# Load order, eviction order and small-step order around the compressed branch of a two-block transformer kernel

## The reference, cut to what matters

```
x = x + 0.5 * swiglu(rms(x, ffn1_norm), ffn1_wg, ffn1_wu, ffn1_wd)
h = rms(x, mix_norm)
q_a, g_a, kc, vc, ks, vs, kw, vw, q_b, k_b, v_b, gate_a, gate_b = split(h @ w_in)
y_a = nsa(q_a, g_a, kc, vc, ks, vs, kw, vw, cmpk_*, cmpv_*) @ w_branch_nsa
y_b = moba(q_b, k_b, v_b) @ w_branch_moba
x = x + (sigmoid(gate_a) * y_a + sigmoid(gate_b) * y_b) @ w_out
x = x + 0.5 * swiglu(rms(x, ffn2_norm), ...)

# in nsa, the compressed branch (k = kc, vc; 2 groups of 64 features):
blocks = windows of 32 tokens, stride 16, + pos_emb
kcb, vcb = gelu(flat(blocks) @ w1) @ w2 ;  kcb = rope(kcb)
p = masked_softmax(q @ kcb * scale);  o_cmp = p @ vcb, weighted by sigmoid(g_a)
```

## Time and profile before

| | |
|---|---|
| median of three runs | 2011.68 us |
| profiled execution, its own time | 2013.12 us |
| its span | 2011.3 us |
| mean granted TensorE clock | 0.976 |
| TensorE busy | 1900.3 us, 94% |
| VectorE busy | 1279.0 us, 64% |
| ScalarE busy | 1100.7 us, 55% |
| GpSimd busy | 109.8 us, 5% |
| DMA | 287.55 MB, mean 143 GB/s |

### The profile page before, as it was taken

One profiled execution on the slowest core, in us unless ns is written; L12 is line 12 of the kernel. 1 busy time (PEld: TensorE's weight loads), 2 busy tenths in 40 slices (PEclk: granted clock), 3 DMA queues, 4 the chain that ended last, 5 costly groups with the idle time before them and its releaser, 6 DMA issues.

```text
span 2011.3 us, 35976 instructions
## 1 busy us (share of the span) xinstructions
PE 1900.3 (94%) x14196; PEld 1694.4 (84%) x14196; DVE 1279.0 (64%) x2078; ACT 1100.7 (55%) x1940; POOL 109.8 (5%) x101
## 2 busy tenths in 40 slices
PE   6999999998799989999989999999999979999997
PEld 4969978876799787888889898889888879898886
DVE  4652354366734667876657587767776647688766
ACT  4372254284534556774446467755774435557753
POOL 3000000004000003200000010001000000010001
PEclk6999999999899999999989999999999979999999
DMA  7231233132223322555442255555554442245544
GB/s 297 95 127 64 103 128 124 66 127 90 79 85 115 103 91 82 188 189 189 158 158 106 85 183 194 188 188 180 181 185 188 155 160 87 104 168 188 187 171 165
DMA packets 41713, 287.55 MB, mean 143 GB/s; under 512 B 4737, under 2 KB 6033, under 8 KB 7793
## 3 DMA queue, kind: packets, MB, share of 16 engines
q1 hardware_dynamic: 39392, 278.15, 38.6%
q0 software_dynamic: 2192, 7.57, 1.1%
HBM read 284.65 MB, written 1.05 MB: 142 GB/s over the span
## 4 chain that ended last, share of the span: by engine, by line
issue 50%; PE 37%; DVE 5%; ACT 4%; POOL 3%; DMA 1%; DVEq 0%; POOLq 0%; ACTq 0%
PE bank L1864 7%; PE bank L1866 7%; PE bank L1865 7%; PE bank L1870 6%; PE bank L1871 3%; PE bank L2002 2%; PE bank L2021 2%; PE bank L1979 1%; ACT work L936 1%; POOL work L760 1%; DVE panels_lo L1272 1%; PE bank L1923 1%; DMA xT<-xin 1%; PE bank L1960 1%; PE bank L2013 1%
## 5 line engine op out<-in xcount | busy, mean ns | idle before, releaser
L1272 DVE TENSOR_TENSOR panels_lo<-raw_panels,panels_hi 128x1024 fp32r<-128x1024 f32 x472 | 581.0, 1248 | 249.2 <-ACT panels_hi L827 247.8
L827 ACT ACTIVATE panels_hi<-raw_panels 128x1024 fp32r<-128x1024 f32 x472 | 488.6, 1054 | 427.6 <-PE bank L1866 279.3
L1870 PE MATMUL bank<-acts,panels_hi 128*128 128x512 f32 x2032 | 714.5, 397 | 3.6 <-DVE xT L1614 1.7
L1871 PE MATMUL bank<-acts,panels_lo 128*128 128x256 f32 x2032 | 568.4, 280 | 0.0
L1870 PEld LDWEIGHTS bank<-acts,panels_hi 128*128 128x128 f32 x2032 | 381.3, 188 | 96.1 <-DVE xT L1614 1.9
L1871 PEld LDWEIGHTS bank<-acts,panels_lo 128*128 128x128 f32 x2032 | 383.3, 189 | 0.2
L1864 PE MATMUL bank<-panels_hi,acts 128*128 128x256 f32 x1024 | 298.8, 292 | 39.5 <-ACT token_major L1164 21.5
L1864 PE MATMUL bank<-acts,panels_hi 128*128 128x256 f32 (+1 forms) x976 | 300.6, 308 | 3.6 <-DVE xT L1614 1.4
L1865 PE MATMUL bank<-acts,panels_hi 128*128 128x256 f32 (+1 forms) x976 | 296.7, 304 | 0.0
L1866 PE MATMUL bank<-acts,panels_lo 128*128 128x256 f32 (+1 forms) x976 | 296.7, 304 | 0.0
L1865 PE MATMUL bank<-panels_lo,acts 128*128 128x256 f32 x1024 | 295.3, 288 | 0.0
(11 more groups left out here) (229 smaller groups left out, 1982.1 us busy)
## 6 DMA issues: line engine op xcount, KB each, us to landing
raw_panels<-weights SPq DMA_DIRECT2D x262, 1024.0 KB, 4.8
near_bias<-rpb POOLq DMA_DIRECT2D x16, 256.0 KB, 3.0
gates<-weights SPq DMA_DIRECT2D x2, 1024.0 KB, 10.5
xT<-xin POOLq DMA_DIRECT2D x4, 512.0 KB, 12.5
out<-xT SPq DMA_DIRECT2D x4, 256.0 KB, 2.2
gates<-consts POOLq DMA_DIRECT2D x1, 448.0 KB, 4.5
consts_sb<-consts POOLq DMA_DIRECT2D x1, 356.0 KB, 3.3
raw_panels<-weights SPq DMA_DIRECT2D x2, 128.0 KB, 2.3
```

The lines of the kernel that those rows point to most:

```text
L827: act.activation(slot_hi(n, a, b), raw_of(n, a, b), ACT.Copy).then_inc(hi_ready, 1)
L1272: dve.tensor_tensor(slot_lo(n, a, b), raw_of(n, a, b), slot_hi(n, a, b).bitcast(F32), ALU.subtract).then_inc(lo_ready, 1)
L1870: pe.matmul(bank.rearrange("p (c t) -> p c t", c=2), whi_, with_rest(xhi_), start=start, stop=False, skip_group_check=True)
L1871: return pe.matmul(bank[:, 0:T], wlo_, xhi_, start=False, stop=stop, skip_group_check=True)
```

## The change

There are four edits. SyncE's loop takes two neighbouring pairs of panels in exchanged order: kv0+2 is waited for before kv0+1, and m0 before kv0+3, so that m0 is loaded before kv0+3 and m0+2 before m0+1. ScalarE evicts `nsa_kv` 0 and `compress(0)` ahead of rounding m0, and `moba_qkv` 0, the compressed keys and `compress_gelu(1)` ahead of rounding m0+2. VectorE rotates the compressed keys ahead of the split of m0+2 and the low parts of the queries, and runs the second half of the compressed softmax ahead of the low parts of the `moba` queries and the split of m0+6. TensorE turns the token scale into columns ahead of the branch gates' product.

```
+        def freeing_order():
+            order = list(range(START2["panels"], START2["panels"] + L["panels"]))
+            for n in sorted(PLAIN - {NSA_G}):
+                i = order.index(n)
+                order[i:i + 2] = [n + 1, n]
+            return order
...
-            for n in range(START2["panels"], START2["panels"] + L["panels"]):
+            for n in freeing_order():
...
 # ScalarE
-            tokens("nsa_kv", 0, [m0])
+            tokens("nsa_kv", 0, [])
             compress_out(0)
+            round_panel(m0)
             tokens("nsa_kv", 1, [])
             compress_out(1)
             compress_gelu(0)
             b = TWO["turn_nsa"].at["turns"]
-            tokens("moba_qkv", 0, [m0 + 1, m0 + 2])
-            compress_gelu(1)
+            tokens("moba_qkv", 0, [m0 + 1])
             act.wait_ge(cm_pe, now(cm_pe, 1))
             act.activation(kct[0:32, 0:HD], banks[7][0:32, 0:HD], ACT.Copy).then_inc(cm_act, 1)
+            compress_gelu(1)
+            round_panel(m0 + 2)
...
 # VectorE
             split_panel(m0 + 1)
             b = TWO["turn_nsa"].at["turns"]
-            for tt in range(TT):
-                turns_lo(b + tt, b + tt - 2, q_turned(0, tt), q_turned(1, tt), HD ** -0.5)
-            split_panel(m0 + 2)
             dve.wait_ge(cm_act, now(cm_act, 1))
             rope(kct[0:32, 0:HD], kct[0:32, P:2 * P], 1, ...)
             dve.sem_inc(cm_dve, 1)
+            split_panel(m0 + 2)
+            for tt in range(TT):
+                turns_lo(b + tt, b + tt - 2, q_turned(0, tt), q_turned(1, tt), HD ** -0.5)
             split_panel(m0 + 3)
...
             b = TWO["turn_moba"].at["turns"]
-            for tt in range(TT):
-                turns_lo(b + tt, b + tt - 2, q_turned(0, TT + tt), q_turned(1, TT + tt), HD ** -0.5)
-            split_panel(m0 + 6)
             dve.wait_ge(cm_act, now(cm_act, 3))
...
             dve.tensor_tensor(heads, heads, bcast(cstat[:, 0:16], 2, NCMP), ALU.mult).then_inc(cm_dve, 1)
+            for tt in range(TT):
+                turns_lo(b + tt, b + tt - 2, q_turned(0, TT + tt), q_turned(1, TT + tt), HD ** -0.5)
+            split_panel(m0 + 6)
...
 # TensorE
             tok_panels("cmp_kv")
+            pe.wait_ge(rs_ready, now(rs_ready, 2))
+            for tt in range(TT):
+                o = pe.matmul(banks[7][:, T + 2 * tt:T + 2 * tt + 2], rs[:, tt * P:(tt + 1) * P], ident[:, 0:2], ...)
+            o.then_inc(rcol_turned, 1)
             n, s = TWO["nsa_g"].at["panels"], TWO["nsa_g"].at["steps"]
             take(s)
...
             o.then_inc(tick, 1)
-            pe.wait_ge(rs_ready, now(rs_ready, 2))
-            for tt in range(TT):
-                o = pe.matmul(banks[7][:, T + 2 * tt:T + 2 * tt + 2], rs[:, tt * P:(tt + 1) * P], ident[:, 0:2], ...)
-            o.then_inc(rcol_turned, 1)
```

More of the change, by code:

```diff
@@ L2238, in _ @@
             tok_panels("cmp_kv")
+            pe.wait_ge(rs_ready, now(rs_ready, 2))
+            for tt in range(TT):
+                o = pe.matmul(banks[7][:, T + 2 * tt:T + 2 * tt + 2], rs[:, tt * P:(tt + 1) * P], ident[:, 0:2],
+                              start=True, stop=True, skip_group_check=True)
+            o.then_inc(rcol_turned, 1)
             n, s = TWO["nsa_g"].at["panels"], TWO["nsa_g"].at["steps"]
@@ L2249, in _ @@
             o.then_inc(tick, 1)
-            pe.wait_ge(rs_ready, now(rs_ready, 2))
-            for tt in range(TT):
-                o = pe.matmul(banks[7][:, T + 2 * tt:T + 2 * tt + 2], rs[:, tt * P:(tt + 1) * P], ident[:, 0:2],
-                              start=True, stop=True, skip_group_check=True)
-            o.then_inc(rcol_turned, 1)
             def compress(j):
```

## The result

The changed kernel takes 1989.86 us, median of four runs (1986.45 to 1993.27), beside 2014.12 us for the kernel before in the same rounds (2008.0 to 2017.09): a ratio of 0.9878, 95% interval 0.9858 to 0.9898, some 24 us or 1.2% faster. A second set of rounds gave 1986.79 us beside 2011.84, ratio 0.988 (0.9855 to 0.9905). The profiled execution took 1988.07 us, its span is 1986.3 us, and the mean granted clock 0.982.

A forecast was written before the change was run, and what follows sets the result against it. TensorE, busy 94% of the span, was taken as the bound. Gains of 10.8 + 9.8, 1.1 + 2.4, 2.8 and 2 x 0.8 make 28.5 us, less 3.4 for new falls: 25, so 1987 us median, range 1980 to 1997.

The forecast's parts named there:

- The chain load, rounding, eviction, TensorE: Before `nsa_kv` 2: m0's late load holds its rounding, that the eviction, that TensorE; a 10.1 us wait in layer 1.
- The new waits: TensorE would newly wait on loads before `compress(1)` and `moba_qkv` 1, 1.5 to 2.2 us each.
- the walk: Step-by-step timing of loads, splits and evictions in both layers: `moba_qkv` 1 starts 10.8 and 9.8 us earlier.
- The wait before `compress(0)`: In layer 2, `compress(0)` is held by the eviction of `nsa_q` 1 behind the rounding of kv0+2, ending at 1606.3.
- The token scale: Turned before the branch-gate product: TensorE's 1.2 us wait goes, but loads of q0+1 and kv0 are issued 0.6 us later.
- The second pair works against the change: m0+1, needed a step before m0+2, is loaded after it; in the old order layer 1's 2.1 us wait would go.
- Compressed keys and softmax: Waits of 1.1 and 2.4 us on the compressed keys go, and the softmax edit gains 0.8 us a layer.
- Clock: Layer 2's falls to half clock go, gaining 2.8 us; new falls after the new waits cost 3.4, bounds 0 and 6.8.
- The waits move to the loads: Rival, chance 0.19: slow load pairs turn the long wait into two waits a layer; gain 18.3 or 16 us, time 1995.
- The ring of loads: Rival, chance 0.05: m0+1's load waits for m0's rounding and split, so steps run in series; 2013 to 2020 us.

The follow-up runs named there:

- the changed kernel's second trace: The changed kernel, no further edit, profiled again in a second set of rounds: 1986.79 us, ratio 0.9880 to the kernel before.
- without the small steps: Changed kernel with VectorE's old order, and ScalarE's compressed-keys copy and `moba_qkv` 0 eviction again behind rounding m0+2: 1991.50 us, ratio 0.9885.
- the kernel of the table's last row: Changed kernel with only the first load pair exchanged, TensorE's edit undone, `moba_qkv` 5 eviction and probabilities copy ahead of rounding m0+7: 1979.06 us, ratio 0.9833.

## Why the prediction was right

- *The chain load, rounding, eviction, TensorE.* This mechanism was right, and shown from both ends: moving the eviction alone gives 19.6 us of the stretches, moving the load alone 16.0.
- *The new waits.* All where the walk had them. `compress(1)` waits 1.3 and 1.55 us (1.5 and 1.7 forecast), `moba_qkv` 1 3.1 and 3.3 us (2.1 and 2.2). `moba_qkv` 1 starts 42.6 and 44.0 us into the stretch; the walk had 41.2 and 42.6. It is 1.4 us late in both layers. In layer 1 half of it is there when m0 is issued: kv0, the second of its pair, landed 11.4 us into the stretch (989.63), 1.4 us later than before (988.61, 10.0 us into it) and not 0.6, and each later load hangs on the split of the one before. By the runs above this goes with TensorE's edit and is no chance. In layer 2 m0's issue was only 0.3 us late. The rest is in the later landings: 8.4 and 8.6 us for the pair of m0+2 and m0+1, where I took 7.9.
- *The wait before `compress(0)`.* Seen for layer 2 (an eviction behind the rounding of kv0+2), missed for layer 1, where it is 0.75 us.
- *The token scale.* The loads slip by 0.35 us, not by the 0.6 us forecast; the turn takes less of TensorE's time than the row's length.
- *The second pair works against the change.* Right: without it 155.7 us instead of 164.9 or 158.6. Both pairs together are worth nothing that can be told beside the eviction; the first alone is.
- *Compressed keys and softmax.* The waits went, and the gate product starts 3.16 us after the end of `moba_qkv` 5 (1056.12 to 1059.28), as forecast (3.15). But the size was off: 1.1 + 2.4 + 1.6 = 5.1 us forecast, some 3 us measured (1.5 a layer). The 1.11 and 2.44 us went with the 10 us wait: with the eviction alone no wait stands there in either layer. I had booked as the gain of these edits what the first edit brings by itself.
- *Clock.* 3.4 us taken for new falls, 6.8 at most. The first trace has three falls, one after each wait before `moba_qkv` 1 and one after the score products. From `moba_qkv` 1 to the gate product a layer takes 36.9 us without a fall, 38.4 with one and 39.9 with two, so a fall costs 1.5 us and the three 4.5. In the second trace there are two. One, in layer 2, follows the 1.93 us wait before `compress(1)`; it makes TensorE late for `moba_qkv` 1 by about what it would have waited there, as forecast for a fall after the first wait of a layer. Over all traces two things come out. First, the length of a wait does not decide alone. Of the 13 waits of 1.9 to 3.3 us in the stretches of all traces ten have a fall beside them; those of 2.17 and 2.22 us in the changed kernel's second trace, and one of 3.09 us without the small steps, have none. Of the shorter ones of 1.1 to 1.6 us one has (1.21 us, in the kernel of the table's last row). Second, the fall after the 24 small score products, which the prediction had only in its upper bound, comes with no idle time before it, in 16 of the 28 stretches, and is as dear. The two falls of layer 2 in the changed kernel's first trace make 3.0 of the 6.3 us that it lies above the second there; the other 3.3 are the later start of `moba_qkv` 1.
- *The sum.* 25 us forecast; 21.5 and 27.8 us by the two traces of the stretches, 24.3 and 25.1 us by the medians. By the first traces of both, 17.6 of the 20.6 us forecast came before `moba_qkv` 1 and 3.9 of the 4.5 behind it. The other 3.5 of the 25.0 us between the two spans are outside the stretches, 3.2 of them in the last pass, for which the forecast had no term. With the changed kernel's second trace, which has fewer falls, the two parts are 20.9 and 6.9 us. So that the forecast hits so closely is partly luck: the small steps were booked 2 us too high, the landings took 3 us from the walk in the first trace, and the pace of the last pass made up for it.
- *Rivals.* "The waits move to the loads" happened in mild form: two waits on loads a layer, with pairs that took 7.6 to 8.6 us. The ring of loads did not turn on itself: m0+1 landed 10 us before the point from which that rival decides.

## What to carry to other kernels

Where one engine both frees banks for TensorE and prepares operands that wait for transfers, put the freeing first: one rounding moved behind two evictions gave most of this change, seven to nine tenths. When a loader with a few places is put into the order in which places come free, check each exchanged pair against the order of use; the pair whose first panel was needed later took back much or all of what the other pair gave. And ask of every small wait in a trace whether it is its own or the echo of the large one before it, before its removal is booked as a gain.

## What the runs showed of the hardware that I had not expected

TensorE's pace in the up and down passes differs from one pass to the next, with a granted clock of 1.00 throughout. The products there come in pairs, one with 512 columns and one with 256. There are four such passes in the second block. From the start of the longer product to the next one it takes 236 ns in some passes, 231.6 in others, and in five of the 56 passes of all traces 230. In 40 us of the last pass (columns as in the earlier trace rows) the kernel before did this in its first trace:

```profile
1860.00:1900.00 40.00, 40.00 (x229) 34.67 (x228) 30.96 (x43) 29.56 (x44) 0.00 (x0) 1.00 0.52 185
```

and the same kernel this in its second:

```profile
1860.00:1900.00 40.00, 40.00 (x233) 35.01 (x232) 31.55 (x44) 30.16 (x44) 0.00 (x0) 1.00 0.55 194
```

229 products against 233. The pace holds for a whole pass of 182 or 185 us and cost the first trace of before 3.2 us there, which are the better part of the 3.5 us that the stretches do not explain. It differs between two executions of one kernel, so the change did not set it. I did not find what does; the third pass ran at 236 ns in all 14 traces. By an estimate from these passes (some 3 us each, in three of the four) it can account for a good part of the spread between runs of one kernel (8.6 us over eleven runs of the kernel before, 16.6 over six of the changed one), but only the profiled executions show their pace. A stretch of the trace is free of this. It has its own scatter, 1.2 us between the two traces of the kernel before but 6.3 us between those of the changed kernel, so differences of a few microseconds between single traces are not shown by it either, unless the waits and falls behind them are read one by one.
